# Expert weights of a mixture-of-experts stage: from one staging buffer to a place of its own for each of two experts

## The chip, the cores and the metric

One core of one Trainium2 chip runs the whole program. The metric is the device time of one execution in microseconds; lower is better. Times below are the median of repeated runs; the profile is of one more execution.

## What is computed

A bidirectional encoder block on 2048 tokens of width 1024: a normalisation, an input projection, a linear recurrence and a long convolution side by side, an output projection, then a mixture of experts, then a last normalisation. The change touches the mixture only. In the reference it is, per token, the best of 4 groups and the best two of its 8 experts:

```python
def expert_block(args):
    xblk, e = args                      # 128 tokens, number of the expert
    a = jax.nn.silu(xblk @ w1[e]) * (xblk @ w3[e])
    return a @ w2[e]
yb = lax.map(expert_block, (xb, block_e)).reshape(n_slots, d)
y = zeros.at[sorted_tok].add(yb[dest] * sorted_gate[:, None])
```

There are 32 experts; w1 and w3 are 1024 x 512 and w2 is 512 x 1024, float32, 6.3 MB for each expert. The tokens of one expert are padded to blocks of 128. With the inputs used, 17 experts have two blocks and 15 have one, 49 blocks in all.

## The kernel before

The stage is written by `experts` (L1758). Products are made in float32r, with each operand split in a high part (rounded) and a low part (what the rounding lost), so each product of a pair is three matmuls: high by high, high by low, low by high (`products`, L1919 to 1922). The weights of an expert therefore go three steps: DMA into a float32 staging buffer, ACT copies them rounded into the high tile, DVE or POOL subtracts high from raw into the low tile.

The buffers: `raw` (`w_raw`, L1783, 12 slabs of 128 x 1024, one expert), `wh` (high and low of w1/w3 for one expert, L1786), `wy` (high and low of w2 for two experts, L1788). One expert is cut in 6 "pairs": pairs 0 to 3 are two k-slices of w1 and w3 together, pairs 4 and 5 are half of w2 each. Each pair is two DMAs of 512 KB. `split_w` of ACT (L1988) makes the high parts of all 6 pairs, `split_w` of DVE (L2043) the low parts of pairs 0 to 4, `split_last` of POOL (L1883) the low part of pair 5.

The order on each engine is the order of its program; semaphores join them.

- SP (L1838 to 1853) only issues the weight loads. A pair of expert e is loaded when the low part of the same pair of expert e-1 is made (`lowered`, `lowered_last`), since both use the same place in `raw`.
- TensorE, per block B (`body`, L1947): the 48 products of block B with w1 and w3 into p1 and p3 (each k counts `used` up by one), then `y(B)`, which makes the 24 products with w2 for the block before (`y_done` up by one at the end; it starts at BASE + 1), then four turns of `a`. `y` waits for the low part of a, for `y_evac` (the former result is copied out), and for w2's low parts.
- ACT, per block (L2010): the high part of turned a, the two copies of y's result to `yb` scaled by the weight (these wait for `y_added`, from POOL), Silu of p1, the high part of the next block's x. After the last block of an expert, `split_w` of the next expert: six copies of 1.9 us each, and the next block's work only behind them.
- DVE, per block (L2061): the low part of a, the turn of the gathered x (`turn`), a = p3 * Silu, the low part of x. After the last block of an expert, the five low parts of the next expert.
- POOL, per block (L1899): the scatter of y's result with accumulation in HBM, the gather of x in four quarters for the block two ahead, then the wait for the scatter (`added`). After the last block of an expert, `split_last` of the next.

`nblk` holds the number of blocks of each expert (row 0) and the running sum through each (row 1). POOL's DMAs write their descriptors to a space of SBUF, whose size is an argument where the program is built (L2220), left at its default. The helper `in_place` (L85) makes a float32r tile and a float32 tile on the same bytes. `final_norm` (L2073) and the routing that comes before the experts (`route`, L1570) put their own tiles over the expert buffers by the offsets in `marks`.

Of the kernel before, what the change touches and what calls it, by code (L numbers as in the profile page):

```python
# [11 lines left out]
P = 128  # L12
SEQ, D = 2048, 1024
CH = 512
KC = D // P
# [10 lines left out]
NT = 16  # L26
# [1731 lines left out]
def experts(nc, dram, ident, marks):  # L1758
# [5 lines left out]
    with ExitStack() as ctx:  # L1764
# [5 lines left out]
        raw_in = [sem(f"raw_in{r}") for r in range(PAIRS)]  # L1770
# [11 lines left out]
        marks["raw_at"] = -(-nc.sbuf_base // 32) * 32  # L1782
        raw = sb("w_raw", [P, SLABS, D])  # L1783
        slabs = raw.rearrange("p s d -> p (s d)").rearrange("p (r c t f) -> p r c t f", c=2, t=2, f=D_EXP)
        marks["wh_at"] = -(-nc.sbuf_base // 32) * 32
        wh = [sb("wh_hi", [P, KC, D], F32R), sb("wh_lo", [P, KC, D], F32R)]  # L1786
        marks["wy_at"] = nc.sbuf_base
        wy = [sb("wy_hi", [P, 2 * FT, D], F32R), sb("wy_lo", [P, 2 * FT, D], F32R)]  # L1788
# [5 lines left out]
        s1, a = sb("s1", [P, D_EXP]), sb("a", [P, D_EXP])  # L1794
# [9 lines left out]
        by_part = lambda w, j: w[:, j:j + 2, :].rearrange("p t (c f) -> p c t f", c=2)  # L1804
        by_j = lambda x: x.rearrange("p k (j b) -> p k j b", j=4)
        def per_block(eng, name, body, following=None, on=lambda e, r: None):
# [5 lines left out]
            def blocks_of(e, r):  # L1812
                n = eng.value_load(nblk[0:1, 0, ds(e, 1)], min_val=1, max_val=NT)
                with eng.Fori(0, n):
                    body(e, eng.snap(B))
                    on(e, r)
                    eng.reg_add(B, B, 1)
# [20 lines left out]
        def _(sp):  # L1838
            with sp.Fori(0, N_EXP) as e:
                for pair in range(PAIRS):  # L1840
                    if pair < D_PAIRS:
                        sp.wait_ge(lowered, BASE + (e - 1) * D_PAIRS + pair + 1)
                    else:
                        sp.wait_ge(lowered_last, BASE + e)
                    j = 2 * pair
                    if pair < H_PAIRS:
                        for c, name in enumerate(("exp_w1", "exp_w3")):
                            src = dram[name].rearrange("o e (p k) f -> p (o e) k f", p=P)[:, ds(e, 1), j:j + 2]
                            sp.dma_start(slabs[:, pair, c], src.rearrange("p a k f -> p (a k) f")).then_inc(raw_in[pair], 16)
                    else:  # L1850
                        for k in (j - KC, j - KC + 1):
# [379 lines left out]
```

## Time and profile before

| | us |
|---|---|
| median of 3 runs | 2207.25 (2206.99 to 2207.91) |
| profiled execution | 2216.69 |
| its span, first to last instruction | 2214.9 |
| TensorE busy | 1995.7 (90%) |
| VectorE, ScalarE, GpSimd busy | 1212.4, 1063.1, 817.7 |
| experts' products with w1/w3, three kinds | 313.2 + 307.7 + 307.4 |
| mean granted TensorE clock | 0.952 of full speed |

PE is TensorE, DVE VectorE, ACT ScalarE, POOL GpSimd; SPq is the queue on which SP issues DMAs. "[3.65 <-DVE wh_lo L2048]" behind an instruction says that its engine was idle for 3.65 us before it, and that this line's instruction ended the wait. Times of a line are the start from the begin of the span, then the duration. A busy time of matmuls counts overlapping ones once. The experts run from about 1290 to 2160 us of the span; the chain of work that ended last is PE's for 28 of 100 parts, on line 1921, which is the matmul of `products`.

### The profile page before, as it was taken

Reading aid. Unit: us, or ns where it says so; the run is one execution under the profiler, and the core shown is the slowest. Engines: PE = TensorE matmul, PEld = TensorE weight load, DVE = VectorE, ACT = ScalarE, POOL = GpSimd, SP = SyncE. Lnnn points to the kernel's source line nnn. Section 1 sums busy time; section 2 is a strip of 40 time slices with the busy share of each in tenths; the row PEclk is TensorE's granted clock in tenths of the full one; section 3 lists DMA queues with packets and bytes.
Section 4 is the critical chain, followed back from the end, with each engine's and each line's share of the span. In section 5 each row is a group of like instructions: output and inputs, shape, how many; then the busy total and the mean of one; then the engine's idle time right before and its main releaser. Section 6 shows DMA issues by size and latency. Waiting matters only on the chain. (4 is left out here: it accounts for less than half of the span.)

```text
span 2214.9 us, 29378 instructions
## 1 busy us (share of the span) xinstructions
PE 1995.7 (90%) x8823; PEld 1404.3 (63%) x8824; DVE 1212.4 (55%) x1133; ACT 1063.1 (48%) x1283; POOL 817.7 (37%) x526
## 2 busy tenths in 40 slices
PE   3999999999999977979999389999898999999980
PEld 2436778777666322327777268888686888888870
DVE  6653223234667734744444655566767666665644
ACT  6871222226556332433333244555757556555634
POOL 0690000000000320322222055576867866675750
PEclk9999999999999998989999679999999999999995
DMA  6691222321234987957443358788989987887848
GB/s 218 238 327 39 76 67 76 95 76 41 50 79 137 348 310 301 347 196 238 169 152 105 143 171 277 218 307 291 370 287 371 376 286 249 306 291 224 304 132 322
DMA packets 206334, 476.88 MB, mean 215 GB/s; under 512 B 23569, under 2 KB 86165, under 8 KB 201111
## 3 DMA queue, kind: packets, MB, share of 16 engines
q1 hardware_dynamic: 165080, 383.61, 47.3%
q0 software_dynamic: 17824, 58.79, 11.6%
q10 hardware_dynamic: 23360, 33.56, 4.8%
q8 instruction: 43, 0.70, 0.1%
q14 instruction: 27, 0.22, 0.0%
HBM read 355.25 MB, written 114.29 MB: 212 GB/s over the span
## 5 line engine op out<-in xcount | busy, mean ns | idle before, releaser
L1921 PE MATMUL p<-wh_hi,x_hi 128*128 128x512 f32 x768 | 313.2, 408 | 22.2 <-DVE wh_lo L2048 14.2
L1867 POOL DMA_INDIRECT xg<-scratch_H,curidx x196 | 285.3, 1456 | 89.8 <-issue 44.8
L1921 PE MATMUL p<-wh_lo,x_hi 128*128 128x512 f32 x768 | 307.7, 401 | 0.0
L1921 PE MATMUL p<-wh_hi,x_lo 128*128 128x512 f32 x768 | 307.4, 400 | 0.0
L2048 DVE TENSOR_TENSOR wh_lo<-w_raw,wh_hi 128x2048 fp32r<-128x2048 f32 x128 | 284.7, 2285 | 26.1 <-ACT wh_hi L1996 26.1
L540 PE MATMUL ps<-h_hi,wp_hi 128*128 128x512 f32 x640 | 257.6, 403 | 4.3 <-DVE wp_lo L735 4.3
L540 PE MATMUL ps<-h_lo,wp_hi 128*128 128x512 f32 x640 | 254.3, 397 | 0.0
L540 PE MATMUL ps<-h_hi,wp_lo 128*128 128x512 f32 x640 | 254.3, 397 | 0.0
L1996 ACT ACTIVATE wh_hi<-w_raw 128x2048 fp32r<-128x2048 f32 x128 | 234.0, 1903 | 0.0
L1886 POOL TENSOR_TENSOR wy_lo<-w_raw,wy_hi 128x2048 fp32r<-128x2048 f32 x32 | 187.7, 5865 | 90.8 <-ACT wy_hi L1999 90.5
L1921 PEld LDWEIGHTS p<-wh_hi,x_hi 128*128 128x128 f32 x768 | 147.0, 191 | 59.1 <-DVE wh_lo L2048 15.8
L1921 PEld LDWEIGHTS p<-wh_hi,x_lo 128*128 128x128 f32 x768 | 147.1, 192 | 35.5
L1921 PEld LDWEIGHTS p<-wh_lo,x_hi 128*128 128x128 f32 x768 | 147.4, 192 | 33.1
L1921 PE MATMUL pyy<-wy_hi,a_hi 128*128 x392 | 156.1, 398 | 5.6 <-ACT yb L1985 5.6
L1921 PE MATMUL pyy<-wy_hi,a_lo 128*128 x392 | 156.0, 398 | 0.0
L1921 PE MATMUL pyy<-wy_lo,a_hi 128*128 x392 | 155.8, 397 | 0.0
L2036 DVE STREAM_TRANSPOSE xT<-xg 128x1024 f32<-128x1024 f32 x49 | 60.8, 1241 | 169.6 <-DMA xg<-scratch_H,curidx 163.8
L540 PEld LDWEIGHTS ps<-h_hi,wp_hi 128*128 128x128 f32 x640 | 121.1, 189 | 45.4 <-ACT hraw L619 6.8
L518 POOL DMA_DIRECT2D xraw<-hc x6 | 3.1, 514 | 390.3 <-DVE hc L743 390.3
L540 PEld LDWEIGHTS ps<-h_hi,wp_lo 128*128 128x128 f32 x640 | 121.1, 189 | 29.1
L540 PEld LDWEIGHTS ps<-h_lo,wp_hi 128*128 128x128 f32 x640 | 121.2, 189 | 28.1 <-issue 0.2
L619 ACT ACTIVATE hraw<-ps 128x512 f32<-128x512 f32 x48 | 28.7, 598 | 213.5 <-PE ps L540 213.5
(329 smaller groups left out, 3588.8 us busy)
## 6 DMA issues: line engine op xcount, KB each, us to landing
w_raw<-in_exp_w_dram SPq DMA_DIRECT2D x384, 512.0 KB, 7.5
dec<-in_decay_dram SPq DMA_DIRECT2D x32, 512.0 KB, 5.5
scratch_KA<-work SPq DMA_DIRECT2D x32, 512.0 KB, 4.5
scratch_SI<-arena SPq DMA_DIRECT2D x32, 512.0 KB, 4.5
kin<-scratch_KA SPq DMA_DIRECT2D x21, 512.0 KB, 7.5
arena<-scratch_SA SPq DMA_DIRECT2D x21, 512.0 KB, 6.0
wp_raw<-in_w_in_dram SPq DMA_DIRECT2D x18, 512.0 KB, 3.8
h_raw<-in_x_dram ACTq DMA_DIRECT2D x4, 2048.0 KB, 15.3
```

What stands on the lines that cost most here:

```text
L518: pool.dma_start(out[halves[h]], a[halves[1 - h]]).then_inc(done, 16)
L540: last = pe.matmul(out, w[:, s, k, :], h, start=(k == 0 and i == 0), stop=(k == KC - 1 and i == 2))
L619: ins = act.activation(out[:, 512 * n:512 * (n + 1)], pj[n], func)
L1867: pool.indirect_dma_start(out=xg[:, j, :], out_offset=None, in_=quarter_rows, in_offset=bass.IndirectOffsetOnAxis(ap=cur[:, j:j + 1], axis ...
L1886: pool.tensor_tensor(lo, raw[:, SLABS - 2:SLABS, :], hi.bitcast(F32), ALU.subtract).then_inc(lowered_last, 1)
L1921: mm = pe.matmul(acc[:, :], x[:, k, :], w, start=(k == 0 and i == 0), stop=(k == n - 1 and i == 2))
L1996: act.activation(by_part(wh[0], j), slabs[:, pair], ACT.Copy).then_inc(rounded, 1)
L2036: dve.transpose(xT[:, :], xg.rearrange("p j d -> p (j d)")).then_inc(trx, 1)
L2048: dve.tensor_tensor(by_part(wh[1], j), slabs[:, pair], by_part(wh[0], j).bitcast(F32), ALU.subtract).then_inc(lowered, 1)
```

## The change

Every one of two experts in turn (r = 0 and 1, even and odd) has its own place for all three of its weights. The staging buffer is gone: the raw weights land on the bytes of the low tile (`in_place`), and the low part is written over them. The high tile of w1/w3 is doubled. SP no longer waits for `lowered` but for TensorE: a w1/w3 pair of expert e+2 is loaded when the last block of expert e has used that pair (`used`, counted by the running block sum, `ends_of`), and w2 of expert e+2 when y of e's last block is done (`y_done`). The order on SP is: expert 0; after the routing's `idx_set` and the landing of the first gather, expert 1; w1/w3 of expert 2; then in turn w1/w3 of expert e+3 and w2 of expert e+2, e from 0. ACT's waits for `used` and `y_done` in `split_w` go. The tile `s1` goes; Silu writes into `a`. The space for POOL's descriptors is set to 2048 bytes. `final_norm` and `route` place their tiles by the new offsets.

```diff
-        raw_in = [sem(f"raw_in{r}") for r in range(PAIRS)]
+        raw_in = [[sem(f"raw_in{r}_{pair}") for pair in range(PAIRS)] for r in range(2)]
...
-        raw = sb("w_raw", [P, SLABS, D])
-        slabs = raw.rearrange("p s d -> p (s d)").rearrange("p (r c t f) -> p r c t f", c=2, t=2, f=D_EXP)
-        wh = [sb("wh_hi", [P, KC, D], F32R), sb("wh_lo", [P, KC, D], F32R)]
-        wy = [sb("wy_hi", [P, 2 * FT, D], F32R), sb("wy_lo", [P, 2 * FT, D], F32R)]
+        wh_lo, wh_raw = in_place(nc, ctx, "wh", [P, 2, H_PAIRS, 4, D_EXP])
+        wy_lo, wy_raw = in_place(nc, ctx, "wy", [P, 2 * FT, D])
+        wh_hi = sb("wh_hi", [P, 2, H_PAIRS, 4, D_EXP], F32R)
+        wy_hi = sb("wy_hi", [P, 2 * FT, D], F32R)
...
         def _(sp):
-            with sp.Fori(0, N_EXP) as e:
-                for pair in range(PAIRS):
-                    if pair < D_PAIRS:
-                        sp.wait_ge(lowered, BASE + (e - 1) * D_PAIRS + pair + 1)
-                    else:
-                        sp.wait_ge(lowered_last, BASE + e)
...
+            def load_h(e, r, ends=None):
+                for pair in range(H_PAIRS):
+                    if ends is not None:
+                        sp.wait_ge(used, BASE + ends * KC + 2 * pair + 2 - KC)
+                    for c, name in enumerate(("exp_w1", "exp_w3")):
+                        src = dram[name].rearrange("o e (p k) f -> p (o e) k f", p=P)[:, ds(e, 1), 2 * pair:2 * pair + 2]
+                        sp.dma_start(wh_raw[:, r, pair, 2 * c:2 * c + 2, :].rearrange("p a f -> p (a f)"), src.rearrange("p a k f -> p (a k) f")).then_inc(raw_in[r][pair], 16)
+
+            def load_y(e, r, ends=None):
+                if ends is not None:
+                    sp.wait_ge(y_done, BASE + ends + 2)
+                for k in range(FT):
+                    src = dram["exp_w2"].rearrange("o e (k p) f -> p (o e) k f", p=P)[:, ds(e, 1), k]
+                    sp.dma_start(wy_raw[:, r * FT + k, :], src.rearrange("p a f -> p (a f)")).then_inc(raw_in[r][H_PAIRS + k // 2], 16)
+
+            def ends_of(e):
+                return sp.value_load(nblk[0:1, 1, ds(e, 1)], min_val=1, max_val=N_BLOCKS)
+
+            load_h(0, 0)
+            load_y(0, 0)
+            sp.wait_ge(marks["idx_set"], BASE + 2)
+            sp.wait_ge(xg_in, 64)
+            load_h(1, 1)
+            load_y(1, 1)
+            load_h(2, 0, ends_of(0))
+            with sp.Fori(0, N_EXP // 2 - 2) as e2:
+                for r in range(2):
+                    load_h(e2 * 2 + r + 3, 1 - r, ends_of(e2 * 2 + r + 1))
+                    load_y(e2 * 2 + r + 2, r, ends_of(e2 * 2 + r))
+            load_h(N_EXP - 1, 1, ends_of(N_EXP - 3))
+            load_y(N_EXP - 2, 0, ends_of(N_EXP - 4))
+            load_y(N_EXP - 1, 1, ends_of(N_EXP - 3))
...
                 for pair in some:
-                    j = 2 * pair
-                    act.wait_ge(raw_in[pair], BASE + (e + 1) * 32)
+                    act.wait_ge(raw_in[r][pair], BASE + (e - r) * 16 + 32)
                     if pair < H_PAIRS:
-                        act.wait_ge(used, BASE + B * KC + j + 2 - KC)
-                        act.activation(by_part(wh[0], j), slabs[:, pair], ACT.Copy).then_inc(rounded, 1)
+                        hi, raw = (w[:, r, pair] for w in (wh_hi, wh_raw))
                     else:
-                        act.wait_ge(y_done, BASE + B + 1)
-                        act.activation(wy[0][:, r * FT + j - KC:r * FT + j - KC + 2, :], raw[:, j:j + 2, :], ACT.Copy).then_inc(rounded, 1)
+                        hi, raw = (w[:, r * FT + 2 * (pair - H_PAIRS):r * FT + 2 * (pair - H_PAIRS) + 2, :] for w in (wy_hi, wy_raw))
+                    act.activation(hi, raw, ACT.Copy).then_inc(rounded, 1)
...
-    nc = _bacc.Bacc("TRN2", target_bir_lowering=False, num_devices=1)
+    nc = _bacc.Bacc("TRN2", target_bir_lowering=False, num_devices=1, dynamic_dma_scratch_size=2048)
```

## Rows read from the trace of the kernel before

**Rows 1.** Busy us (and count) of PE, PEld, DVE, ACT, POOL; clock; DMA share; GB/s
```profile
1300.00:1350.00 50.00, 50.00 (x222) 40.39 (x221) 22.77 (x20) 19.95 (x22) 27.91 (x23) 1.00 0.76 240
1600.00:1700.00 100.00, 96.41 (x416) 77.59 (x415) 68.64 (x49) 64.17 (x59) 72.46 (x41) 0.98 0.92 328
```

**Rows 2.** Waits of PE, 1350 to 2150 us: us in total, times, longest
```profile
PE p L1921 <- DVE wh_lo L2048: 14.2, 4, 3.7
```

**Rows 3.** Timeline of ACT: start, us, instruction, idle before it
```profile
1304.38 0.60 ACT L2015 ACTIVATE s<-p 128x512 f32<-128x512 f32 x1 [5.82 <-PE p L1921]
...
1529.20 0.60 ACT L2015 ACTIVATE s<-p 128x512 f32<-128x512 f32 x1 [3.24 <-PE p L1921]
1537.95 3.70 ACT L1999 ACTIVATE wy_hi<-w_raw 128x2048 fp32r<-128x2048 f32 x2
...
1542.39 1.27 ACT L1985 ACTIVATE yb<-pyy,weight 128x512 f32<-128x512 f32 x2 [0.25 <-issue]
1546.53 0.60 ACT L2015 ACTIVATE s<-p 128x512 f32<-128x512 f32 x1 [2.88 <-PE p L1921]
1550.85 1.16 ACT L1973 ACTIVATE x_hi<-xT 128x512 fp32r<-128x512 f32 x2 [3.72 <-DVE xT L2036]
...
1568.99 0.60 ACT L2015 ACTIVATE s<-p 128x512 f32<-128x512 f32 x1 [4.54 <-PE p L1921]
...
2140.43 0.60 ACT L2015 ACTIVATE s<-p 128x512 f32<-128x512 f32 x1 [3.23 <-PE p L1921]
```

**Rows 4.** Timeline of DVE and of PE in the same interval
```profile
1549.57 1.25 DVE L2036 STREAM_TRANSPOSE xT<-xg 128x1024 f32<-128x1024 f32 x1 [5.19 <-DMA xg<-scratch_H,curidx]
...
1556.19 0.79 PE L1921 MATMUL p<-wh_hi,x_hi 128*128 128x512 f32 x1 [3.65 <-DVE wh_lo L2048]
```

**Rows 5.** Timeline of POOL
```profile
1524.41 6.53 POOL L1886 TENSOR_TENSOR wy_lo<-w_raw,wy_hi 128x2048 fp32r<-128x2048 f32 x1 [5.95 <-ACT wy_hi L1999]
...
1532.37 1.62 POOL L1880 DMA_INDIRECT scratch_X<-yb,curspot  x1 [0.82 <-POOL curspot L1877]
...
1542.70 1.89 POOL L1867 DMA_INDIRECT xg<-scratch_H,curidx  x1 [0.31 <-issue]
1544.62 4.63 POOL L1886 TENSOR_TENSOR wy_lo<-w_raw,wy_hi 128x2048 fp32r<-128x2048 f32 x1
```

**Rows 6.** Timeline of SP's DMA queue
```profile
1535.14 7.41 SPq L1849 DMA_DIRECT2D w_raw<-in_exp_w_dram  x8
```

**Rows 7.** Four-us windows (columns as rows 1) after S = 1442.65, a single's end
```profile
1446.60:1450.60 4.00, 4.00 (x20) 3.23 (x20) 4.00 (x3) 4.00 (x3) 3.20 (x3) 1.00 1.02 292
...
1454.60:1458.60 4.00, 4.00 (x18) 3.20 (x17) 3.22 (x3) 2.14 (x4) 3.67 (x3) 1.00 1.03 419
```

**Rows 8.** Issue to landing: issued 1243.2-1245.1; 1396.7-1399.4; 1450.8-1451.3
```profile
DMA to landing us min/median/max: 9.9/10.8/11.8
...
DMA to landing us min/median/max: 5.3/5.9/6.5
...
DMA to landing us min/median/max: 7.9/8.5/9.0
```

**Rows 9.** Timeline of POOL where it pauses between gathers
```profile
1619.79 0.95 POOL L1867 DMA_INDIRECT xg<-scratch_H,curidx  x1 [3.62 <-DMA scratch_X<-yb,curspot]
...
1954.14 2.15 POOL L1867 DMA_INDIRECT xg<-scratch_H,curidx  x1 [3.04 <-issue]
```

**Rows 10.** Timelines at the start: SP, POOL, DVE
```profile
1279.48 16.49 SPq L1849 DMA_DIRECT2D w_raw<-in_exp_w_dram  x8
1280.42 1.90 POOL L1859 DMA_INDIRECT xg<-scratch_H,idx  x1 [0.30 <-issue]
...
1287.30 1.25 DVE L2036 STREAM_TRANSPOSE xT<-xg 128x1024 f32<-128x1024 f32 x1 [5.79 <-DMA xg<-scratch_H,idx]
...
1310.92 0.96 POOL L1867 DMA_INDIRECT xg<-scratch_H,curidx  x1 [0.30 <-issue]
...
1314.02 1.25 DVE L2036 STREAM_TRANSPOSE xT<-xg 128x1024 f32<-128x1024 f32 x1 [2.27 <-DMA xg<-scratch_H,curidx]
```

More of the change, by code:

```diff
@@ L1884, in split_last @@
                 pool.wait_ge(rounded, BASE + e * PAIRS + PAIRS)
-                hi, lo = (v[:, r * FT + 2:r * FT + 4, :] for v in wy)
-                pool.tensor_tensor(lo, raw[:, SLABS - 2:SLABS, :], hi.bitcast(F32), ALU.subtract).then_inc(lowered_last, 1)
+                hi, lo, raw = (v[:, r * FT + 2:r * FT + 4, :] for v in (wy_hi, wy_lo, wy_raw))
+                pool.tensor_tensor(lo, raw, hi.bitcast(F32), ALU.subtract).then_inc(lowered_last, 1)
             def added(B):
@@ L1939, in y @@
                     for c in range(2):
-                        whi, wlo = (w[:, ds(place + k, 1), c * 512:(c + 1) * 512].rearrange("p a n -> p (a n)") for w in wy)
+                        whi, wlo = (w[:, ds(place + k, 1), c * 512:(c + 1) * 512].rearrange("p a n -> p (a n)") for w in (wy_hi, wy_lo))
                         mm = products(py[c], a_hi, a_lo, k, whi, wlo, FT)
@@ L1945, in _, with body @@
             transpose_a()
-            def body(e, B):
+            def body(e, B, r):
                 pe.wait_ge(a_ready, BASE + B + 1)
@@ L1953, in body @@
                         pe.wait_ge(lowered, BASE + e * D_PAIRS + k // 2 + 1)
-                    for acc, cols in ((p1, slice(0, D_EXP)), (p3, slice(D_EXP, 2 * D_EXP))):
-                        mm = products(acc, x_hi, x_lo, k, wh[0][:, k, cols], wh[1][:, k, cols], KC)
+                    for c, acc in enumerate((p1, p3)):
+                        whi, wlo = (w[:, r, k // 2, 2 * c + k % 2, :] for w in (wh_hi, wh_lo))
+                        mm = products(acc, x_hi, x_lo, k, whi, wlo, KC)
                     mm.then_inc(used, 1)
@@ L2006, in _ @@
             act.wait_ge(a_ready, BASE + 1)
-            act.activation(s1[:, 0:1], a[:, 0:1], ACT.Silu).then_inc(act_passed, 1)
+            act.activation(yb[:, 0:1], a[:, 0:1], ACT.Silu).then_inc(act_passed, 1)
             act.wait_ge(act_passed, BASE + 1)
@@ L2014, in body @@
                 act.wait_ge(a_ready, BASE + B + 1)
-                act.activation(s1[:, :], p1[:, :], ACT.Silu).then_inc(s_ready, 1)
+                act.activation(a[:, :], p1[:, :], ACT.Silu).then_inc(s_ready, 1)
                 split_x(B + 1)
@@ L2047, in split_w @@
                     if pair < H_PAIRS:
-                        dve.tensor_tensor(by_part(wh[1], j), slabs[:, pair], by_part(wh[0], j).bitcast(F32), ALU.subtract).then_inc(lowered, 1)
+                        dve.tensor_tensor(wh_lo[:, r, pair], wh_raw[:, r, pair], wh_hi[:, r, pair].bitcast(F32), ALU.subtract).then_inc(lowered, 1)
                     else:
-                        hi, lo = (v[:, r * FT + j - KC:r * FT + j - KC + 2, :] for v in wy)
-                        dve.tensor_tensor(lo, raw[:, j:j + 2, :], hi.bitcast(F32), ALU.subtract).then_inc(lowered, 1)
+                        hi, lo, raw = (v[:, r * FT + j - KC:r * FT + j - KC + 2, :] for v in (wy_hi, wy_lo, wy_raw))
+                        dve.tensor_tensor(lo, raw, hi.bitcast(F32), ALU.subtract).then_inc(lowered, 1)
             dve.memset(a[:, :], 0.0).then_inc(a_ready, 1)
```

33 lines of the change are left out of this document (13 added, 20 removed).

## The prediction

> **What bounds the kernel now.** I read the windows by stage first. From 1300 to 2160 us the expert stage runs, and TensorE is busy for all of the windows at its ends and for 96 of 100 us in the middle, while the DMA engines are busy 76% at first and 92% in the middle [rows 1]. So the stage is nearly TensorE's own work, with losses in one part. The waits of TensorE name them: four waits, 14.2 us, for the low parts of w1/w3 (wh_lo), none longer than 3.7 us [rows 2]. The Silu of ACT marks the end of each block's first products (I call this instant S). An undisturbed interval is 1546.53 - 1529.20 = 17.33 us [rows 3]. From the first Silu to the one at 2140.43 there are 47 intervals: 836.05 - 47 x 17.33 = 21.5 us above an undisturbed stage [rows 3]. Four intervals (22.5, 22.6, 22.6 and 23.6 us) have **22.0 us** of it alone; the others are 17.33 or a little less. The lost time exceeds the 14.2 us of idle, because TensorE restarts slowly (0.79 us for the first product after the idle [rows 4], where one takes 0.4 in the steady state).
>
> What caused them? Not a late weight. In the stalled interval ACT's first idle is before x_hi, 3.72 us, for the turned x [rows 3], and DVE's turn starts at 1549.57, when the gathered x has landed [rows 4]. The last gather was issued only at 1542.70 to 1544.59, because POOL first had wy_lo (6.53 us), then the scatter, then four gathers of about 1.9 us [rows 5]. POOL's cycle is about 20 us (1524.41 to 1544.62) against TensorE's 17.33. This happens only where several experts in a row have one block each. From the Silu and wh_hi times, 15 of the 32 experts have one block (number 4, 7 to 10, 12 to 17, 19, 22, 25, 28); 17 have two. DMA is full too in such a run: of four-us windows one has 292 GB/s, the next but one 419 [rows 7].
>
> **The change part by part.**
> *Instructions of the splits.* Same shapes, same count, contiguous instead of strided; ACT's waits on `used` and `y_done` in its split_w were already satisfied, since it stands behind a Silu that waits for the whole block. I take nothing for both. A strided row beside a contiguous one is not in the trace; +-1% of ACT's 1.9 us per split would be hidden by the idle that it has before each Silu.
>
> *Silu into a instead of s1.* Its readers, the turns of the previous a, are done before the Silu's block ends. Nothing.
>
> *Start.* Before, SP issues the first pair of expert 1 at 1279.48, as soon as the first low part exists, while POOL issues the first gather. The last quarter is issued by 1282.32 and turned at 1287.30: 5.0 us. Without loads beside it the same step takes 1314.02 - 1311.88 = 2.1 us [rows 10]. Now expert 1 is loaded only after that gather. TensorE starts on this x, so **-2.8 us** (bounds 0 and -3.5). Expert 1 itself isn't needed before 1321, and its 6.3 MB take some 19 us.
>
> *Loads of w1/w3.* Before, SP loads expert f+2's first pair when DVE has lowered f+1's, 5.9 us after S (1535.14) [rows 6]. Now a pair goes when TensorE has used expert f's: 8.4, 5.6, 2.8 and 0 us before S of f's last block. They come 6 to 14 us earlier, but no wait of before was for them. Gain nothing.
>
> *Loads of w2: the new wait.* SP now waits for y_done of expert f-1's last block before it loads w2 of f+1. That y is made in the first block of f, behind f's own products. If f has two blocks it is long over. If f has one block, y comes after S(f): 24 of the 72 products, 5.6 us, so SP issues at S+5.65. ACT wants the first of these pairs at S+8.75 (1537.95 - 1529.20) and had finished both at S+12.45 [rows 3]. Queued behind ACT's wait are a_hi and the two yb copies (about 1.8 us in all), and TensorE's next y waits for these. Its due time is S+17.1. With X the time from SP's issue to the landing of the last of the four 512 KB transfers, the next y starts at S + 5.65 + X + 1.9 + 1.85 = S + 9.4 + X, and the stall is **X - 7.7 us for each single-block expert**. Behind SP's wait are the w1/w3 loads of f+3, which aren't due.
> X from both sides: the opening burst of 12 such transfers, issued from 1238.29 on with nothing beside them, has its last four landing up to 11.8 us after issue: 6.3 MB in 18.6 us; two pairs on a free queue land 5.9 us after issue [rows 8]. That is about 3.2 us and 2.1 MB / 0.41 = 5.1 us: X = 8.3. The other bound: two pairs issued from S+5.9 at 1448.6, at exactly the place of the new loads, have the last at 1451.3 + 9.0 = 1460.3: X = 11.7 [rows 8]; these had two other w2 transfers just ahead of them, which the new ones have not. In that part of the cycle POOL's scatter and gathers share the engines and the rate is 292 GB/s instead of 419 [rows 7]. With 6.35 us at the first rate and the rest of 2.1 + 0.7 MB at the second, plus the tail, I take **X = 10**, stall 2.3 us. The bounds give 0.6 and 4.0.
> The Trainium skill ("DMA: Bandwidth & Descriptors", section "Anatomy of one DMA — SWDGE (gpsimd) path") fits a transfer by 2.0 us and bytes / 436 GB/s. As an estimate from it, 2.1 MB would take 6.8 us, below 7.7, and no expert would stall. The opening burst ran at 18.6 us for 6.3 MB where that fit has 16.4, so the trace is slower already without company.
>
> *The same wait on POOL.* POOL's wy_lo waits for ACT's last w2 split, so its chain starts later: S+17.6 plus the stall, not S+12.45. From its start to the turn of the gathered x it needs 25.2 us (1524.41 to 1549.57) when DVE's splits lie beside it; part of it would now run while DVE is idle (wy_lo 4.63 instead of 6.53 us [rows 5]): I take 20. That x is due at S + 2 x 17.33 - 0.7 plus two stalls D: D + 17.6 + 20 = 34.0 + 2D, D = 3.6; since with longer cycles the queue is emptier, I take 3.3. That binds inside a run, where a single stands between singles: 6 of the 15 (numbers 8, 9, 13 to 16). For the other 9 the 2.3 us hold.
>
> *Descriptor space.* The POOL queue's space is cut from its default to 2048 bytes (the build line of the diff). In the trace POOL pauses between gathers at 1619.79 (3.62 us) and 19 blocks later at 1954.14 (3.04 us), each time until the scatter before it has landed [rows 9]. If this is a full ring, and the space is an eighth, the pause comes every 2.4 blocks. It costs 0 to 3.6 us of POOL, free where an expert has two blocks (POOL idles there 6 us before wy_lo), and in a run I count 1 us more in all, with 0 and 20 (8 blocks by 2.5 us) as bounds.
> The Trainium skill ("SBUF — State Buffer", section "SBUF size: 192, 224, or 256?") calls these 16 KiB of a partition the descriptor ring of POOL's DMAs. By that reading the pauses are the ring's; the 19 blocks between the two agree with a ring that fills, and nothing in the trace shows the small one.
>
> **Sum.** Stalls after: 9 x 2.3 + 6 x 3.3 = 40.5 us; ring 1. Before: 22.0, which these replace, since late x and late w2 lie one after the other on the same cycle and only the later counts. Start -2.8. 40.5 + 1 - 22.0 - 2.8 = +16.7 us. The profiled execution of before took 2216.69 us (span 2214.9), 9.4 above the median of the runs; the profile would go to 2233.4 (span 2231.6), and the median to 2207.25 + 16.7 = **2224 us**.
>
> **The rivals.**
> (1) *The w2 loads land nearly in time* (X = 8.3, as with a free queue). For it: the loads of w1/w3 are done earlier, and the DMA queue is emptier at S+5.65 than before. Against it: scatter and gathers stand in the same 8 us. 9 x 0.6 = 5.4, and in runs POOL still binds with about 1.9 (the sum of D = 3.6, less 1.7): 6 x 1.9 = 11.4. 16.8 - 22 - 2.8 = -8.0 us: 2199.
> (2) *No stall at all*, by the skill's fit, X = 6.8, and POOL's chain not later than before: 2207.25 - 2.8 - 22 = 2182. Against it: 7.3 MB for each single take 17.4 us even at 419 GB/s and 25 at 292 [rows 7], so in a run DMA alone keeps some of the loss.
> (3) *The change costs nothing and brings nothing in the runs*: there DMA sets the pace in both kernels and the 22 us stay; the 5 isolated singles stall 0.6: 2207.25 + 3.0 - 2.8 = 2207.5. For it: the DMA share is 0.92 over 300 us [rows 1].
> (4) *Worse than forecast: the stalls also cost slow restarts*, as those of before did (3.65 us idle, 5.1 us lost [rows 3, 4]; the granted clock is 0.98 over that stretch instead of 1.00 [rows 1], part of it at the lower level of 1.2 GHz). X = 11.7 and 15 stalls of 4, each 1.5 dearer: 82.5 - 22 - 2.8 = +57.7: 2265. It decides from idles of some 3 us on.
> (5) *The ring alone*: w2 lands in time, but the pauses fall on POOL's chain in the runs (12 blocks at 1 us each), which is the one that stalls now: 2207.25 - 2.8 + 12 = 2216.5, slower.
>
> **How the numbers follow.** Forecast 0.49, rival 1 0.10, rival 2 0.05, rival 3 0.12, rival 4 0.12, rival 5 0.12. Rival 1 gives 0.02 to "same", since some of it lies within 0.2%. 0.2% is 4.4 us, about what a measurement here tells from no change. Slower 0.73, same 0.14, faster 0.13. The range takes in rival 1 at its lower end and reaches half way to rival 4: 2199 to 2245; it leaves out rival 2 and the harder half of rival 4.
>
> **What would show it.** In the after profile: ACT waiting for the DMA of w2 (wy_hi) once for each single-block expert, some 2 us or more each (0.2 us in all now); TensorE waiting before y (pyy) for ACT's yb, not before wh; the four 3.7 us waits gone or turned into shorter ones; POOL pauses near a scatter's landing every second or third block; the first turn of x near 1284.5. Wrong if X is under 8, which ACT's waits would show directly; the start is wrong if the first turn stays at 1287.

## The result and the profile of the changed kernel

| | before | after |
|---|---|---|
| median, range (6 runs each) | 2207.6 us (2207.0 to 2210.7) | 2300.8 us (2289.6 to 2305.7) |
| the profiled execution; its span | 2216.69; 2214.9 | 2300.18; 2298.4 |
| first Silu of the experts | 1304.38 | 1296.88 |
| 47 intervals from there | 836.05 | 927.28 |
| of it above 47 x 17.33 us | 21.5 | 112.8 |

The ratio is 1.0404, with a 95% interval of [1.0391, 1.0417]. The forecast was 2224 (2199 to 2245). The sign was right and the size wrong: +93.2 us where +16.7 was forecast.

From trace to trace the change is 83.5 us; the profiled run of before lay 9.1 above the median of its six, that of after 0.7 below. The table accounts for it: the first Silu comes 7.5 us earlier and the 47 intervals take 91.2 us longer. All that was lost was lost in the expert stage. Of the 7.5 us, 3.1 lie before the first gather of x (1273.30 against 1270.24). That point varies from 1269.0 to 1274.5 over the traces of all kernels here, so these 3.1 are not put down to the change.

The traces also set a count right: they have 48 Silus and 768 products of each kind with w1/w3, 16 for each block, so there are 48 blocks and not 49. The last expert (number 31) has one block as well: 16 experts have one block and 16 have two. No expert follows it, so the 15 stalls of the forecast's sum are not touched.

Two stretches of after, in the columns of [rows 1]:

```profile
1300.00:1350.00 50.00, 50.00 (x222) 40.31 (x221) 22.43 (x21) 20.95 (x25) 24.91 (x22) 1.00 0.67 199
1600.00:1700.00 100.00, 86.83 (x365) 68.45 (x365) 65.28 (x44) 60.92 (x54) 64.83 (x39) 0.97 0.85 296
```

At the front nothing is lost. In the middle TensorE is busy 86.83 us instead of 96.41, and the DMA share is down from 0.92 to 0.85: the weights are the same bytes, spread over a longer time. The waits of after, of the whole trace (us in total, times, longest):

```profile
POOL wy_lo L1905 <- ACT wy_hi L2015: 174.4, 30, 11.3
ACT wy_hi L2015 <- DMA wy_raw<-in_exp_w_dram: 156.4, 58, 7.1
...
PE pyy L1940 <- ACT yb L2005: 77.5, 29, 5.7
...
PE p L1940 <- DVE wh_lo L2064: 4.9, 4, 3.5
PE p L1940 <- DVE x_lo L2046: 4.7, 1, 4.7
```

ACT waited 0.2 us in all for w2 before, and now 156.4. It waits 58 times, twice for nearly every expert. TensorE's four waits for wh_lo [rows 2] have almost gone; in their place stand 29 waits before y. One of them, 5.67 us, is before the very last y, which before has too (5.64 us). The other 28, 71.8 us in all, are stalls at the end of an expert: 14 behind a one-block expert and 14 behind a two-block one. One of these, after the Silu at S = 1348.68, first SP's queue and then ACT:

```profile
1340.43 9.30 SPq L1847 DMA_DIRECT2D wh_raw<-in_exp_w_dram  x8
1350.66 1.90 SPq L1854 DMA_DIRECT2D wy_raw<-in_exp_w_dram  x4
```
```profile
1348.68 0.60 ACT L2031 ACTIVATE a<-p 128x512 f32<-128x512 f32 x1 [5.42 <-PE p L1940]
...
1350.21 7.32 ACT L2015 ACTIVATE wh_hi<-wh_raw 128x2048 fp32r<-128x2048 f32 x4
1362.12 1.92 ACT L2015 ACTIVATE wy_hi<-wy_raw 128x2048 fp32r<-128x2048 f32 x1 [4.59 <-DMA wy_raw<-in_exp_w_dram]
1364.44 1.92 ACT L2015 ACTIVATE wy_hi<-wy_raw 128x2048 fp32r<-128x2048 f32 x1 [0.41 <-DMA wy_raw<-in_exp_w_dram]
1366.27 0.58 ACT L1998 ACTIVATE a_hi<-pta 128x512 fp32r<-128x512 f32 x1
1366.74 1.26 ACT L2005 ACTIVATE yb<-pyy,weight 128x512 f32<-128x512 f32 x2
1367.88 0.61 ACT L2031 ACTIVATE a<-p 128x512 f32<-128x512 f32 x1
```

Let f be the expert that ends at S; the w2 here is that of f + 1. What it waits for, y of the last block of f - 1, had been done in the block before, more than ten us earlier (e3 below shows when). But in SP's program the w1/w3 loads of f + 2 stand ahead of it, and these are released pair by pair only as TensorE goes through f's *last* block, up to S itself. So w2 is issued at S + 2.0, right behind 4.2 MB of its own queue. The last transfer lands 13.8 us later, and a_hi and yb, for which TensorE's next y waits, stand behind ACT's wait for it.

TensorE, and its granted clock in windows of one us (columns as in [rows 1]), at the end of this stall:

```profile
1368.64 0.50 PE L1940 MATMUL pyy<-wy_hi,a_hi 128*128 x1 [2.68 <-ACT yb L2005]
1368.97 0.50 PE L1940 MATMUL pyy<-wy_lo,a_hi 128*128 x1
...
1370.55 0.63 PE L1940 MATMUL pyy<-wy_hi,a_lo 128*128 x1
1370.98 0.63 PE L1940 MATMUL pyy<-wy_hi,a_hi 128*128 x1
```
```profile
1368.00:1369.00 1.00, 0.36 (x2) 0.37 (x3) 0.96 (x2) 0.73 (x3) 1.00 (x1) 1.00 0.00 0
1370.00:1371.00 1.00, 1.00 (x4) 0.72 (x4) 1.00 (x1) 0.00 (x0) 1.00 (x2) 0.50 0.00 0
1371.00:1372.00 1.00, 1.00 (x4) 0.81 (x3) 1.00 (x2) 0.00 (x0) 0.60 (x2) 0.50 0.00 0
1373.00:1374.00 1.00, 1.00 (x6) 0.79 (x5) 0.00 (x0) 0.00 (x0) 1.00 (x2) 1.00 0.00 0
```

After 2.68 us of idle the clock is granted at 0.50, that is 1.2 GHz, for some 3 us, and the products start 0.43 us apart, against 0.23 at full clock. The two intervals around it measure 19.20 and 19.84 us, together 4.38 above two undisturbed ones: 2.68 idle and 1.7 for the clock. In the stage TensorE has 30 idles of over 0.7 us, 76.1 us together; behind 17 of them one-us windows stand at 0.50, for about 3 us in most cases and about 6 in the longest. 112.8 - 76.1 = **36.7 us** are lost beyond the idle. The clock accounts for most of that: the one-us windows from the first Silu to the last add up to some 68 us at 0.50 (17 in before), and at 0.43 instead of 0.23 us from product to product that is 31 us, an estimate. The length of the idle alone does not tell whether the clock falls. Behind the first of these two it stayed at 1.00, behind the second it fell to 0.50:

```profile
1630.33 0.49 PE L1940 MATMUL pyy<-wy_hi,a_hi 128*128 x1 [3.06 <-ACT yb L2005]
2187.76 0.50 PE L1940 MATMUL pyy<-wy_hi,a_hi 128*128 x1 [1.88 <-ACT yb L2005]
```

The loss can be told apart by the kind of expert. I take a cycle of TensorE from its first product of one block to that of the next, and count what it has above 17.33 us:

| behind the end of | before | after | e3 (below) |
|---|---|---|---|
| a two-block expert, 15 cycles | -0.4 | 42.1 | -0.6 |
| a one-block expert, 15 cycles | 22.3 | 70.0 | 67.5 |
| the other 17 cycles | 2.3 | 2.1 | 8.2 |

The columns add up to 1 to 3 us more than the intervals lose, since they take in the first block of all.

A one-block expert, S = 1443.25, SP and then ACT:

```profile
1449.89 1.92 SPq L1854 DMA_DIRECT2D wy_raw<-in_exp_w_dram  x4
```
```profile
1456.03 1.91 ACT L2015 ACTIVATE wy_hi<-wy_raw 128x2048 fp32r<-128x2048 f32 x1 [3.53 <-DMA wy_raw<-in_exp_w_dram]
1461.78 1.91 ACT L2015 ACTIVATE wy_hi<-wy_raw 128x2048 fp32r<-128x2048 f32 x1 [3.84 <-DMA wy_raw<-in_exp_w_dram]
```

Here the release itself is late (S + 6.6, against S + 5.65 in the forecast), since TensorE idled 1.59 us before the y that it waits for (at 1444.01). The second pair is in hand 1461.78 - 1449.89 = 11.9 us after the first issue, where I took X = 10. TensorE idles 4.20 us at 1465.97. This is the longest X of the 15: over all of them it is 8.6 to 11.9 us, 10.5 in the mean, and the issue comes at S + 5.6 to S + 9.6, 7.45 in the mean. Behind two-block experts X is 12.5 to 14.1, 13.5 in the mean, from an issue at S + 1.5 to S + 2.1.

The start, DVE:

```profile
1281.06 1.25 DVE L2052 STREAM_TRANSPOSE xT<-xg 128x1024 f32<-128x1024 f32 x1 [2.62 <-DMA xg<-scratch_H,idx]
```

POOL issued the last quarter of that gather from 1277.36 to 1279.26, so the step takes 1.8 us instead of 5.0 [rows 10].

### The profile page after: what moved, and what is told of

It reads as the page before. It is cut to its first block and busy times, and to the rows that moved or that the text cites. A ratio compares the mean times of both kernels' runs of the same rounds, so it can differ in the third digit from the quotient of the medians.

```text
span 2298.4 us, 29276 instructions
## 1 busy us (share of the span) xinstructions
PE 2018.8 (88%) x8823; PEld 1413.1 (61%) x8824; DVE 1247.7 (54%) x1133; ACT 1068.5 (46%) x1283; POOL 794.6 (35%) x526
## 5 line engine op out<-in xcount | busy, mean ns | idle before, releaser
L1886 POOL DMA_INDIRECT xg<-scratch_H,curidx x196 | 278.5, 1421 | 120.0 <-issue 78.4
L2064 DVE TENSOR_TENSOR wh_lo<-wh_raw,wh_hi 128x2048 fp32r<-128x2048 f32 x128 | 284.6, 2283 | 19.0 <-ACT wh_hi L2015 19.0
L1940 PE MATMUL pyy<-wy_hi,a_hi 128*128 x392 | 170.4, 435 | 77.5 <-ACT yb L2005 77.5
L2015 ACT ACTIVATE wh_hi<-wh_raw 128x2048 fp32r<-128x2048 f32 x128 | 234.0, 1901 | 0.0
L1905 POOL TENSOR_TENSOR wy_lo<-wy_raw,wy_hi 128x2048 fp32r<-128x2048 f32 x32 | 150.1, 4691 | 174.5 <-ACT wy_hi L2015 174.4
L2015 ACT ACTIVATE wy_hi<-wy_raw 128x2048 fp32r<-128x2048 f32 x64 | 122.3, 1916 | 156.4 <-DMA wy_raw<-in_exp_w_dram 156.4
L1940 PE MATMUL pyy<-wy_lo,a_hi 128*128 x392 | 165.9, 423 | 0.0
L1940 PE MATMUL pyy<-wy_hi,a_lo 128*128 x392 | 165.7, 423 | 0.0
L1940 PEld LDWEIGHTS pyy<-wy_hi,a_hi 128*128 128x128 f32 x392 | 81.0, 207 | 108.8 <-issue 89.8
```

Source lines behind the costliest of these rows:

```text
L1886: pool.indirect_dma_start(out=xg[:, j, :], out_offset=None, in_=quarter_rows, in_offset=bass.IndirectOffsetOnAxis(ap=cur[:, j:j + 1], axis ...
L1905: pool.tensor_tensor(lo, raw, hi.bitcast(F32), ALU.subtract).then_inc(lowered_last, 1)
L1940: mm = pe.matmul(acc[:, :], x[:, k, :], w, start=(k == 0 and i == 0), stop=(k == n - 1 and i == 2))
L2015: act.activation(hi, raw, ACT.Copy).then_inc(rounded, 1)
L2064: dve.tensor_tensor(wh_lo[:, r, pair], wh_raw[:, r, pair], wh_hi[:, r, pair].bitcast(F32), ALU.subtract).then_inc(lowered, 1)
```

## The experiments

Kernels that ran together share their runs of the kernel before: its median was 2207.6 beside after, 2210.3 beside e1 to e4, 2209.4 beside e5 to e8 and 2208.3 beside e9 to e11. The ratios are taken within a group; a difference of medians across groups is uncertain by about 3 us. "Loss" is the time of the 47 intervals above 47 x 17.33 us in the profiled execution.

| kernel | median us | ratio to before, 95% interval | loss us |
|---|---|---|---|
| before | 2207.6 | 1 | 21.5 |
| after | 2300.8 | 1.0404 [1.0391, 1.0417] | 112.8 |
| e1_ring | 2216.6 | 1.0024 [1.0013, 1.0035] | 23.8 |
| e2_start | 2205.7 | 0.9987 [0.9977, 0.9996] | 17.5 |
| e3_order | 2254.0 | 1.0194 [1.0181, 1.0208] | 73.1 |
| e4_halves | 2239.6 | 1.0128 [1.0113, 1.0142] | 54.5 |
| e5_one_high | 2242.6 | 1.0144 [1.0127, 1.0161] | 55.1 |
| e6_one_high_ring | 2220.3 | 1.0053 [1.0033, 1.0073] | 28.5 |
| e7_after_ring | 2296.1 | 1.0402 [1.0378, 1.0427] | 103.0 |
| e8_half_w2 | 2201.9 | 0.9961 [0.9948, 0.9973] | 14.2 |
| e9_pool_relief | 2245.7 | 1.0163 [1.0146, 1.0180] | 58.6 |
| e10_relief | 2245.2 | 1.0155 [1.0128, 1.0182] | 58.4 |
| e11_before_half | 2184.3 | 0.9887 [0.9870, 0.9905] | -0.2 |

My theory after reading the trace: w2 is late by the *order on SP* in two-block experts and by its *release* in one-block ones; the rivals were the smaller descriptor space, and the other edits.

**Parts of the change alone, on the kernel before.** e1_ring, the descriptor space only:

```diff
-    nc = _bacc.Bacc("TRN2", target_bir_lowering=False, num_devices=1)
+    nc = _bacc.Bacc("TRN2", target_bir_lowering=False, num_devices=1, dynamic_dma_scratch_size=2048)
```

> The kernel before with one change: POOL's descriptor space at 2048 bytes. Theory A (the order and the wait of the w2 loads make the 92 us): the pauses of POOL between gathers, which the trace of after has at the third gather of every second block (1.7 to 3.9 us), appear here too, but a two-block expert hides them; +2 to +12 us, all in the runs of single-block experts. Rival B (the small descriptor space makes the slowdown, by way of late gathers): +60 us or more.

Measured: ratio 1.0024, some 5 us, as theory A had it. Its waits, 1330 to 2230 us:

```profile
POOL xg L1867 <- issue: 93.8, 137, 4.7
...
PE p L1921 <- DVE wh_lo L2048: 17.1, 12, 3.7
```

In the kernel before, the first of these lines has 42.4 us. POOL now pauses every second or third block (20 pauses over 1.2 us in 48 blocks, up to 4.75 us), and TensorE's four waits have become twelve. That is a small part of the 93 us.

e2_start, expert 1 loaded only after the first gather:

```diff
+            load(0)
+            sp.wait_ge(marks["idx_set"], BASE + 2)
+            sp.wait_ge(xg_in, 64)
+            with sp.Fori(1, N_EXP) as e:
+                load(e)
```

> The kernel before, with only the start of the change: SP loads expert 1 after the first gather has landed. The trace of after has the first turn of x 3.1 us and the first Silu 4.4 us earlier, counted from the first gather's issue. If that is this wait alone, this kernel is 3 to 4.5 us faster than before and the stage behind it is unchanged. If the four stalls of before depend on the phase of the loads, it is within 2 us of before.

Measured: 0.13% less than before, 2.9 us by the ratio, with an interval of 0.9 to 5.1; just under the 3 to 4.5 expected. The traces have 31.1 us from the first gather to the first Silu in before, 27.1 here and 26.6 in after. This is the part of the change that gains, and e2_start is the fastest of all kernels here that compute the whole layer.

**The order on SP.** e3_order is the changed kernel with two lines exchanged, in the loop and in the same way behind it:

```diff
-                    load_h(e2 * 2 + r + 3, 1 - r, ends_of(e2 * 2 + r + 1))
                     load_y(e2 * 2 + r + 2, r, ends_of(e2 * 2 + r))
+                    load_h(e2 * 2 + r + 3, 1 - r, ends_of(e2 * 2 + r + 1))
```

> The changed kernel with the two loads of SP's loop exchanged: w2 of expert e+2 first, then w1/w3 of expert e+3. Theory A: w2 then goes during the first block of a two-block expert, so ACT's waits for w2 vanish at all 17 of them, and at the 15 single-block experts they get shorter, since no w1/w3 pair stands ahead in the queue; time 2215 to 2245. Rival B (descriptor space) or rival C (the low part written over the raw part, or the bigger tiles, cost time by themselves): 2285 or more, the ACT waits moved but the time kept.

Measured: 46.8 us less than after, at 2254.0; the direction was as expected, and 9 us were missing to the expected range. The two-block expert shown above, now SP and ACT of e3:

```profile
1336.52 1.97 SPq L1854 DMA_DIRECT2D wy_raw<-in_exp_w_dram  x4
1339.77 9.38 SPq L1847 DMA_DIRECT2D wh_raw<-in_exp_w_dram  x8
```
```profile
1348.01 0.60 ACT L2031 ACTIVATE a<-p 128x512 f32<-128x512 f32 x1 [5.53 <-PE p L1940]
...
1357.34 3.70 ACT L2015 ACTIVATE wy_hi<-wy_raw 128x2048 fp32r<-128x2048 f32 x2
```

w2 is issued 11.5 us before S, both splits follow without a wait, and TensorE's waits before y are 16 instead of 29 (49.8 us in the window 1330 to 2230, 5.86 of them before the last y). The 42.1 us behind two-block experts are gone, all of them: they were the order's. The 70.0 behind one-block experts stay at 67.5, against the expectation that these waits get shorter too. X there is 9.5 to 11.0 us, 10.3 in the mean, though no w1/w3 pair stands ahead of w2 any more.

**The release.** e4_halves, on e3, lets the first two slabs of w2 go when y has used the first two of the old ones:

```diff
+                    if ends is not None and k == 0:
+                        sp.wait_ge(y_half, BASE + ends + 1)
+                    elif ends is not None and k == 2:
+                        sp.wait_ge(y_done, BASE + ends + 2)
...
+                    if k == 1:
+                        mm.then_inc(y_half, 1)
```

> As the run with the loads exchanged, and w2 is released in halves: its first two slices when TensorE has used k = 0 and 1 of the last y, the others at the end of y. Theory A: the first half goes 2.8 us earlier after a single-block expert, so the first wait of ACT shrinks by up to 2.8 us and the second by about 1 (the transfers are limited by their bytes): 5 to 20 us less than with the exchange alone. If the landing of the last transfer is set by DMA's rate alone: within 4 us of it.

Measured: 14.4 us less again. In the same window TensorE's waits before y fall from 49.8 to 14.3 us (5.59 of them before the last y), but its waits for wh_lo rise from 5.5 to 28.5, with losses of 3 to 6 us at the ends of four two-block experts, which had at most 1 in e3. There the gathered x was late. Two things could make it so: the w1/w3 loads, now out before S, or POOL's pauses.

**The descriptor space with the new loads.** To give it 16 KB again, room was needed. e5_one_high is the control: e4 with one place for the high parts of w1/w3.

```diff
-        wh_hi = sb("wh_hi", [P, 2, H_PAIRS, 4, D_EXP], F32R)
+        wh_hi = sb("wh_hi", [P, H_PAIRS, 4, D_EXP], F32R)
...
+                        act.wait_ge(used, BASE + B * KC + 2 * pair + 2 - KC)
+                        hi, raw = wh_hi[:, pair], wh_raw[:, r, pair]
```

> The kernel of e4_halves (the changed kernel, w2 loads queued ahead of the w1/w3 loads and released in two halves; 2239.6 us) with one thing different: the high parts of w1/w3 have one place instead of two, as in the kernel before. ACT's split then waits for TensorE's use of the old high part; it stands behind a Silu that waits for all of that. It is the control for the next run, whose larger ring needs this room. Theory A (that wait never lasts, and where the high parts lie costs nothing): 2236 to 2243 us. Rival B (the second place for the high parts is worth something, ACT's splits wait): above 2246, with ACT idle before wh_hi put down to PE.

Measured: 2242.6, loss 55.1 against 54.5. The second place for the high parts, with the waits that it saved, is worth nothing.

e6_one_high_ring is e5 with the default space:

```diff
-    nc = _bacc.Bacc("TRN2", target_bir_lowering=False, num_devices=1, dynamic_dma_scratch_size=2048)
+    nc = _bacc.Bacc("TRN2", target_bir_lowering=False, num_devices=1)
```

> e5 with POOL's descriptor space at its default again (16 KB a partition, as before the change) instead of 2048 bytes. In e4 TensorE waited 28.5 us for wh_lo behind late gathers, the longest where POOL paused for 4.2 to 4.7 us in the third of four gathers until a scatter landed, while the w1/w3 loads that now go out in the last block filled the DMA queues. Theory A (it takes both: the small ring turns the slow scatter into a late gather): the wait for wh_lo falls to 5 to 15 us, POOL's issue wait from 94 to about 42 us, and the time by 12 to 25 us, to 2215 to 2228. Rival B (the early loads alone delay the gather): the wait for wh_lo stays above 22 us, and the time is within 5 us of e5, as the ring alone cost 5 us in the kernel before (e1_ring).

Measured: 2220.3, 22.3 us less, as theory A said. The same gather in e5, POOL and then DVE:

```profile
1338.91 0.97 POOL L1889 DMA_INDIRECT xg<-scratch_H,curidx  x1 [0.30 <-issue]
1344.40 0.95 POOL L1889 DMA_INDIRECT xg<-scratch_H,curidx  x1 [4.52 <-issue]
```
```profile
1351.83 1.25 DVE L2058 STREAM_TRANSPOSE xT<-xg 128x1024 f32<-128x1024 f32 x1 [12.69 <-DMA xg<-scratch_H,curidx]
```

and in e6:

```profile
1339.32 0.97 POOL L1889 DMA_INDIRECT xg<-scratch_H,curidx  x1 [0.30 <-issue]
1340.59 0.95 POOL L1889 DMA_INDIRECT xg<-scratch_H,curidx  x1 [0.30 <-issue]
```
```profile
1347.74 1.25 DVE L2058 STREAM_TRANSPOSE xT<-xg 128x1024 f32<-128x1024 f32 x1 [8.13 <-DMA xg<-scratch_H,curidx]
```

In e5 the third of four gathers waits 4.52 us, the turn comes after S (1349.02) and the interval takes 22.47 us. In e6 it doesn't wait, the last quarter is out at 1342.79 and takes 4.95 us to the turn, the turn is done before S (1349.49), and the interval is 17.32. But a pause of this size was harmless in e1, the kernel before with the small space. There, POOL and then DVE, with S at 1354.67:

```profile
1349.85 0.94 POOL L1867 DMA_INDIRECT xg<-scratch_H,curidx  x1 [4.33 <-issue]
1351.10 0.95 POOL L1867 DMA_INDIRECT xg<-scratch_H,curidx  x1 [0.30 <-issue]
```
```profile
1354.01 1.25 DVE L2036 STREAM_TRANSPOSE xT<-xg 128x1024 f32<-128x1024 f32 x1 [9.22 <-DMA xg<-scratch_H,curidx]
```

The last quarter is out 2.6 us before S in e1 and 2.4 us before S in e5 (1345.65 + 0.95), so the pause eats as much in both. What differs is the landing: 2.0 us in e1, where no weight is on its way, and 5.2 in e5, where SP has issued eight w1/w3 transfers from 1340.77 to 1349.96. The pause takes the slack, and the landing is long beside the new loads (5.2 us in e5, 4.95 in e6, 2.0 in e1); here only both together make x late. These landings are those of one gather in each kernel. The same small space costs 5 us beside the old loads and 22 beside the new ones.

e7_after_ring gives the unchanged order and waits of after the default space, with the room made in the same way.

> The changed kernel itself (2300.8 us) with one place for the high parts of w1/w3 and the default descriptor space; loads, queue order and waits are those of the change. What of the 93 us is the ring's? Theory A (every block that stalls is held by w2, and POOL's pauses lie beside these stalls): 2290 to 2301 us, TensorE's waits for yb still above 65 us. Rival B (the pauses feed the stalls through scatter, y and the next x): under 2285, TensorE's waits for yb under 60 us.

Measured: 2296.1, waits before y 74.0 us in the window, 5.41 of them before the last y. Theory A: the ratio is that of after within its interval. While w2 is as late as in the change, the pauses lie beside that stall.

**Bytes or latency.** e8_half_w2 loads half of w2's bytes at unchanged places, and DVE and POOL lower only that half; the result is not the layer's. (An expert has 6.3 MB in all, not the 4.4 of the expectation below; w2 has 2.1 of them.)

```diff
-                    sp.dma_start(wy_raw[:, r * FT + k, :], src.rearrange("p a f -> p (a f)")).then_inc(raw_in[r][H_PAIRS + k // 2], 16)
+                    n = D if ends is None else D // 2
+                    sp.dma_start(wy_raw[:, r * FT + k, 0:n], src.rearrange("p a f -> p (a f)")[:, 0:n]).then_inc(raw_in[r][H_PAIRS + k // 2], 16)
```

> The changed kernel with half of the bytes of w2 loaded: 4 transfers of 256 KB for an expert instead of 512 KB, at the same places and behind the same waits. ACT writes the full high part from the half that is there (same shape, the half read twice), DVE and POOL form the low part of that half only (half as long), and TensorE makes the same number of products of the same size; its output isn't the layer's. Theory A (what is late is the bytes: w2 waits for its turn at 300 to 420 GB/s behind w1/w3 transfers of the same bundle): each of the 28 stalls before yb loses 2.5 to 3.2 us, ACT's wait for w2 falls from 156 to under 90 us, and the time to 2215 to 2245. Rival B (fixed latency and the place in SP's order set it, not the bytes): ACT's wait stays above 120 us and the time above 2265. 1 MB in 4.4 MB for each expert less also unloads the rest of the cycle, which both theories share.

Measured: 2201.9, below the range of theory A. Three waits before y are left, 3.9 us (1330 to 2230). In the same one-block expert (S = 1440.78 here) SP issues at 1447.08, and ACT:

```profile
1451.49 3.73 ACT L2021 ACTIVATE wy_hi<-wy_raw 128x2048 fp32r<-128x2048 f32 x2 [1.85 <-DMA wy_raw<-in_exp_w_dram]
```

With half the bytes all four are in hand within 6.3 us instead of 11.9. e11_before_half does the same to e2_start, as a control.

> e2_start (2205.7 us) with half of w2's bytes, exactly as in e8_half_w2: ACT writes the full high part, DVE and POOL form half of the low part, TensorE does the same products; its output isn't the layer's. It is the control for e8, which fell from 2300.8 to 2201.9: how much of that is the unloading of DMA and POOL, which any kernel would have? Theory A (the gain of e8 is w2 landing in time): the kernel before gains only what its four stalls cost, 12 to 22 us: 2184 to 2194, so that e8 still stands 8 to 18 us behind it, with the rest of the changed order's cost. Rival B (everything here follows the DMA's load): it would fall much further, under 2180.

Measured: 2184.3; the loss of the 47 intervals is nil. So the kernel before gains 21.4 us by the lighter load, and the changed one 98.9. With half the bytes they stand 17.6 us apart, with all of them 95.1 (2300.8 - 2205.7): some 77 of the 95 us depend on the size of w2, and 17.6 are left for everything else that differs between the two. How much of this is the transfer and how much the halved low part on DVE and POOL isn't separated.

**An attempt to shorten POOL's chain.** e9_pool_relief moves one of POOL's two slabs to DVE, on e2_start; e10_relief does so on e6.

```diff
-                hi, lo = (v[:, r * FT + 2:r * FT + 4, :] for v in wy)
+                hi, lo = (v[:, r * FT + 3:r * FT + 4, :] for v in wy)
...
+                        n = 2 if pair < D_PAIRS else 1
+                        hi, lo = (v[:, r * FT + j - KC:r * FT + j - KC + n, :] for v in wy)
```

> e2_start (the kernel before, expert 1 loaded after the first gather; 2205.7 us) with POOL lowering only one of w2's four slabs for each expert instead of two; DVE lowers the other, after its own five. POOL's cycle in a run of one-block experts was about 20 us against TensorE's 17.33, of it 6.5 for wy_lo. Theory A (that cycle is what stalls TensorE every few experts): POOL's wy_lo falls to some 3.3 us, its cycle under 17.5, the four stalls of 3.7 us with 22 us lost go, and the time is 2184 to 2191. Rival B (the DMA queues set the pace in such a run; they moved at 92% there): the gathers land no earlier, and the time stays at 2200 to 2206. Rival C (DVE is the next that is late, with 1.1 us more for each expert): new waits for x_lo or wh_lo, 2195 to 2215.

> The same shift of one slab from POOL to DVE on e6_one_high_ring (loads by TensorE's use, w2 first and in halves, default descriptor space; 2220.3 us). What is left there, 44 us in the one-block experts, has two candidates. Theory A (w2 comes too late in a one-block expert, whatever POOL does): TensorE's waits for yb stay at 12 to 16 us, 2213 to 2221. Rival B (what is left is the chain over POOL: late wy_hi, late wy_lo, late scatter and gather): both waits fall to a third, and the time is under 2205.

Measured: 40 and 25 us slower than the kernels that they start from, slower than any theory had it. DVE of e9 around the Silu at 1335.17, and a wait of TensorE:

```profile
1330.12 5.61 DVE L2062 TENSOR_TENSOR wy_lo<-w_raw,wy_hi 128x2048 fp32r<-128x2048 f32 x2
1335.66 0.68 DVE L2051 TENSOR_TENSOR a_lo<-pta,a_hi 128x512 fp32r<-128x512 f32 x1
```
```profile
PE pyy L1929 <- DVE a_lo L2051: 38.9, 25, 1.8
```

a_lo stands behind the added slab, and that slab was priced at 1.1 us and takes three times as long. In the first expert, where POOL isn't at its own slab, both of DVE's take 3.42 us together. At the 31 experts after it the 128x1024 slab alone takes 3.42 us in the mean, and it ends 1.07 to 1.09 us after POOL's slab each time. One of them, POOL and then DVE:

```profile
1666.73 4.28 POOL L1894 TENSOR_TENSOR wy_lo<-w_raw,wy_hi 128x1024 fp32r<-128x1024 f32 x1 [1.56 <-ACT wy_hi L2009]
```
```profile
1668.67 3.42 DVE L2062 TENSOR_TENSOR wy_lo<-w_raw,wy_hi 128x1024 fp32r<-128x1024 f32 x1
```

DVE's slab ends after S, so y stalls at 25 expert ends, now in two-block experts too. A step that comes late was put ahead of a due one in an in-order queue, as in the change itself. Whether a shorter POOL cycle would remove the four stalls of before isn't told by these two runs. In e11 the four are gone, but there both w2's transfers and POOL's piece (3.20 us) are smaller. To move w2's splits on ACT, DVE and POOL behind the block's a_hi, yb and gather wasn't tried; it needs a first block of an expert apart from the others.

## Why the prediction was wrong in size

**What bounds the kernel, and the 22 us of before.** As forecast, TensorE's waits for wh_lo [rows 2] fell to 4.9 us in all, and late w2 took their place. That DMA alone sets the pace in the runs (rival 3) is refuted for the sum, since after loses 91 us more with a lower DMA share. Whether the 22 us of before come from POOL's cycle, as I said, or from the transfers stays open: halving w2 (e11) removes them and lightens both. The count of blocks was wrong by one (16 experts have one block), without effect on the sum, and the DMA share over 300 us is 0.91 where I wrote 0.92.

**Splits, Silu into a.** Taken at nothing. No run has the in-place form alone. ACT's split takes 1.90 us in both kernels, and in e5 the doubled high part and its saved waits are worth nothing that can be told. They are bounded by e6: with the order, half of the release and the space mended, 0.5% remains against before and 0.7% against e2_start, and part of that is still w2.

**Start.** The mechanism was right: the step from gather to turn shrank by 3.2 us in after. The sizes agree by luck in part: -2.8 forecast and -2.9 measured in e2_start, but with an interval of 0.9 to 5.1, and from the first gather to the first Silu the traces gain 3.9 (e2) and 4.4 us (after), more than my bound of 3.5. The trace of e2 also has three long intervals instead of four.

**Loads of w1/w3 "gain nothing".** True as a gain, but wrong as a cost. I asked only whether somebody had waited for these loads. I didn't ask what else they now stand in front of: SP's own w2 loads, and, in e4 and e5, the scatter and gather in the 8 us before S. The forecast even said "Behind SP's wait are the w1/w3 loads of f+3, which aren't due", which reads the queue from one side only. What mattered is what stands *ahead* of w2.

**Two-block experts.** This is the step that failed: "If f has two blocks it is long over." The release is; the issue is not. In the trace of after this costs 42.1 us where I had none, and e3 shows it as the order's: the 42.1 are gone, and the median falls by 46.8 us of the 93.2 for an exchange of two lines.

**One-block experts.** The mechanism was right (issue after S, ACT's wait, a_hi and yb behind it, TensorE before y), and the price too small. X = 10 was close: 10.5 in the mean of the 15. But the working that I gave for it doesn't yield it. 6.35 us at 292 GB/s and the rest of 2.8 MB at 419 are 8.6 us, and 10 needs a tail of 1.4 us that I didn't source; with the 3.2 us of the free queue it would be 11.8. The issue came 1.8 us later than I had it (S + 7.45 in the mean instead of 5.65), where TensorE still idled or ran at the low clock from the expert before. TensorE's idles behind one-block ends are 46.2 us (41.6 before y, 4.6 before the products with w1/w3), not far from the 40.5 of the sum; the cycles lose 70.0. The other 24 us were put at nothing, and they are mostly the slow restarts of the next paragraph. In the case shown above, my own formula puts the next y at S + 9.4 + 11.9 + 1.0 = S + 22.3; it started at S + 22.7 (1465.97). The idle there was 4.20 us and not more, since TensorE came to it late itself. The Trainium skill ("DMA: Bandwidth & Descriptors", section "Anatomy of one DMA — SWDGE (gpsimd) path") has a fit of 2.0 us and bytes / 436 GB/s for one DMA issued by GpSimd, an estimate of 6.8 us here. These four DMAs are issued by SP, beside other traffic; the trace measured 8.6 to 11.9 us for them, and the fit doesn't carry over.

**Slow restarts.** I had them as rival 4 alone, at 1.5 us each, though [rows 4] already showed one. They belong in the sum of every case with stalls of that size: 36.7 us of the loss. With stalls of 2.3 us I took them as free, and wrote that rival 4 decides from some 3 us on. The trace has no such limit: the clock fell to 1.2 GHz behind idles of 1.88 and 2.68 us, and not behind one of 3.06.

**Descriptor space.** Taken at 1 us, bounds 0 and 20; alone it costs 5 (e1), in the changed kernel nothing that can be told (e7), and 22 once w2 is mended (e6). The pause "every 2.4 blocks" was right: 20 in 48 blocks in e1. What I missed is that the pause and the w1/w3 loads add up: in the gather shown, the pause was harmless with a landing of 2 us, and beside the loads, whose move I had priced at nothing, it was 5. The Trainium skill ("SBUF — State Buffer", section "SBUF size: 192, 224, or 256?") takes the 16 KiB for POOL's descriptor ring; e1, e5 and e6 agree, as the pauses between gathers come and go with that size (from 1330 to 2230 us, 93.8 us in e1 and 97.0 in e5, against 42.4 in the kernel before and 45.9 in e6).

**Range.** It reached only half way to rival 4, and no case combined two-block stalls with slow restarts. The two together are the miss: 42.1 us behind two-block experts where I had none, and 70.0 behind one-block ones where I had 40.5. That is 42.1 + 29.5 = 71.6 us, against the 112.8 - 41.5 = 71.3 that the intervals lost beyond my sum. The rest of the 76.5 by which the forecast was short lies outside the intervals and between the profiled executions and the medians.

## What to carry to other kernels

When a load's wait changes, write out the whole queue in program order with the time of every release in it: a load is issued at the latest release of all that stand ahead of it, not at its own. Put the load that is due first, or released first, at the front; here that was two lines and 47 us. And price a stall with what follows it: behind 17 of 30 idles TensorE ran for some 3 us, at most about 6, at 1.2 GHz, and nearly half as much again was lost on top of the 76.1 us of idle.

## What the runs showed of the hardware that was not expected

- The descriptor space costs by what else is queued: the same cut from its default to 2048 bytes costs 5 us (e1), nothing that can be told (e7) or 22 us (e6).
- POOL's low part is not proportional to its size beside a busy DVE. With half the size, in e9:

```profile
1534.07 4.29 POOL L1894 TENSOR_TENSOR wy_lo<-w_raw,wy_hi 128x1024 fp32r<-128x1024 f32 x1 [10.78 <-ACT wy_hi L2009]
```

  while 128x2048 took 4.63 to 6.53 us in [rows 5]. The half-size one was expected to take some 3.3 us. It took 4.24 us in the mean, and 2.54 in the first expert, where DVE isn't at its own; DVE's slab of that size took 3.42 us beside POOL's and 1.22 at its shortest.
- Right behind 4.2 MB of w1/w3 on the same queue, the 2.1 MB of w2 took 12.5 to 14.1 us from the first issue to the last landing; issued some 5 us later, behind one-block experts, they took 8.6 to 11.9. In the case shown for e8, half the bytes took 6.3 us at most.
